# Five stage beginnings of a three-block network, worked row tile by row tile

## What is computed

```python
def rmsnorm_2(x, g):
    xf = x.astype(jnp.float32)
    y = xf * lax.rsqrt(jnp.mean(xf * xf, axis=-1, keepdims=True) + EPS)
    return (y * g.astype(jnp.float32)).astype(x.dtype)

def half_ffn(h, shift, scale, gate, g_pre, g_post, w13, w2):
    u = modulate_2(rmsnorm_2(h, g_pre), shift, scale)
    return h + 0.5 * gate * rmsnorm_2(swiglu(u, w13, w2), g_post)
```

## Time and profile before

| | us |
|---|---|
| median of 3 runs | 2326.73 |
| lowest and highest | 2322.61, 2327.68 |
| the profiled execution's own time | 2324.72 |
| its span, first to last instruction | 2323.3 |
| PE, DVE, ACT, POOL busy | 1982.9, 1008.2, 735.3, 42.6 |

### The profile page before, as it was taken

How to read it: one execution, slowest core, us unless ns; L and a number is a source line. 1 busy time by engine, 2 the same in 40 slices (tenths; PEclk the granted TensorE clock), 3 DMA queues, 4 the chain that set the end, 5 groups by cost and what they waited for, 6 DMA issues and landing times.

```text
span 2323.3 us, 28401 instructions
## 1 busy us (share of the span) xinstructions
PE 1982.9 (85%) x11830; PEld 1311.9 (56%) x11830; DVE 1008.2 (43%) x1713; ACT 735.3 (32%) x1196; POOL 42.6 (2%) x47
## 2 busy tenths in 40 slices
PE   6999777777877887777788799989999899999997
PEld 3556413332332433342444288868999788785786
DVE  3544222221221221222533367666664667653386
ACT  4333211111110111112111144454654554543365
POOL 0000000000000000000000000000000000000010
PEclk8998898989999999888799999999999999999999
DMA  9977999999999999999999955435345555250430
GB/s 399 419 310 264 405 392 410 417 413 414 413 414 414 416 413 412 416 411 408 410 410 409 405 188 192 168 102 170 112 143 175 165 178 185 95 203 19 145 118 19
DMA packets 210432, 672.03 MB, mean 289 GB/s; under 512 B 11504, under 2 KB 134512, under 8 KB 152192
## 3 DMA queue, kind: packets, MB, share of 16 engines
q1 hardware_dynamic: 210304, 670.21, 74.7%
HBM read 669.12 MB, written 1.05 MB: 288 GB/s over the span
## 4 chain that ended last, share of the span: by engine, by line
PE 50%; DMA 34%; DVE 11%; ACT 4%; issue 2%; SPq 0%; POOL 0%; DVEq 0%; ACTq 0%
DMA ring<-in_w 24%; PE pb L231 7%; PE pb L239 7%; PE pb L232 7%; PE pb L233 7%; DMA ring<-in_w_a 6%; PE pb L240 4%; DMA ring<-in_w_in 3%; DVE WB L333 3%; PE pb L1844 3%; PE pb L774 2%; PE pb L1869 2%; ACT WB L327 1%; DMA ring<-in_w_mod 1%; PE pb L3149 1%
## 5 line engine op out<-in xcount | busy, mean ns | idle before, releaser
L333 DVE TENSOR_TENSOR WB<-ring,WB 128x1024 fp32r<-128x1024 f32 (+3 forms) x370 | 426.1, 1193 | 465.4 <-ACT WB L327 465.1
L327 ACT ACTIVATE WB<-ring 128x1024 fp32r<-128x1024 f32 (+3 forms) x370 | 361.6, 1026 | 800.0 <-DMA ring<-in_w_a 463.3
L1844 PE MATMUL pb<-ring,big 128*32 128x512 f32 x2048 | 300.3, 679 | 147.1 <-DMA ring<-in_w 131.5
L231 PE MATMUL pb<-HHL,WB 128*128 128x256 f32 (+1 forms) x976 | 292.8, 300 | 11.8 <-DVE WB L333 4.3
L232 PE MATMUL pb<-HHL,WB 128*128 128x256 f32 (+1 forms) x976 | 284.2, 291 | 0.0
L233 PE MATMUL pb<-HHL,WB 128*128 128x256 f32 (+1 forms) x976 | 283.8, 291 | 0.0
L239 PE MATMUL pb<-HHL,WB 128*128 128x512 f32 x704 | 253.5, 404 | 1.7 <-DVE tmpT L643 1.4
L1844 PEld LDWEIGHTS pb<-ring,big 128*32 128x32 f32 x2048 | 46.8, 114 | 364.0 <-DMA ring<-in_w 275.3
L231 PEld LDWEIGHTS pb<-HHL,WB 128*128 128x128 f32 x976 | 195.1, 200 | 35.9 <-issue 20.6
L1869 PE MATMUL pb<-ring,big 128*32 128x512 f32 x1024 | 163.6, 649 | 49.5 <-DMA ring<-in_w 41.7
L240 PE MATMUL pb<-HHL,WB 128*128 128x256 f32 x704 | 198.9, 283 | 0.0
(11 more groups left out here) (467 smaller groups left out, 2268.2 us busy)
## 6 DMA issues: line engine op xcount, KB each, us to landing
ring<-in_w SPq DMA_DIRECT2D x384, 1024.0 KB, 16.5
ring<-in_w_a SPq DMA_DIRECT2D x66, 1024.0 KB, 13.3
ring<-in_w_in SPq DMA_DIRECT2D x38, 1024.0 KB, 10.0
ring<-in_w_ada SPq DMA_DIRECT2D x36, 1024.0 KB, 9.5
ring<-in_w_b SPq DMA_DIRECT2D x33, 1024.0 KB, 5.0
ring<-in_w_mod SPq DMA_DIRECT2D x24, 1024.0 KB, 11.6
ring<-in_w_out SPq DMA_DIRECT2D x8, 1024.0 KB, 5.2
ring<-in_b_w_in SPq DMA_DIRECT2D x8, 1024.0 KB, 6.3
```

The lines of the kernel that those rows point to most:

```text
L231: pe.matmul(o, l[0], r[0], start=start, stop=False)
L327: act.activation(WB[:, c % 2, 0, x:y], flat[:, x:y], ACT.Copy).then_inc(*A(("high", c, z)))
L333: dve.tensor_tensor(WB[:, c % 2, 1, x:y], flat[:, x:y], WB[:, c % 2, 0, x:y].bitcast(F32), ALU.subtract).then_inc(*V(("low", c, z), *([("f ...
L1844: e = pe.matmul(PB[half][32 * j:32 * j + 32, :], xeT[:, kk, 32 * x:32 * x + 32], s[:, 512 * j:512 * j + 512], start=kk == 0, stop=kk == 7)
```

## The change

At the five places the work is reordered by row tile. Tile 0's sum of squares is made by ACT and DVE in halves, then its norm, its 8 transposes, and eight gain-and-shift operations of 128 tokens each, all on DVE (L656 or L658 of the changed kernel). The high and low parts are made for four blocks at once (512 columns), low parts half by DVE and half by POOL (`low2`, L664). Tile 1 follows. PE multiplies tile 0 with the first chunk while tile 1's norm goes on, then tile 0 with the second chunk (in mx: tile 0 with both chunks first), then tile 1 with both. So the instructions on the first two chunks of fa and fb, on the first of mx and on the first two of b3 move half of the tokens each, and there are twice as many. The low part of the second chunk of each stage is made by POOL (`pool_split_half`, L338) and no longer by DVE. At three of the places the end of the stage before is woven in (`act_cross`, `dve_cross`). The first norm of the final output is also made tile by tile; it keeps its instructions otherwise.

```diff
-    def both_columns(pe, bank, hi, lo, kk):
-        pe.matmul(bank[:, :].rearrange("p (z t) -> p z t", z=2), hi, HHL[:, :, kk, 0:256], start=kk == 0, stop=False)
-        return pe.matmul(bank[:, 0:256], lo, HH[:, kk, 0:256], start=False, stop=kk == 7)
+    def both_columns(pe, bank, hi, lo, kk, x=0, n=256):
+        pe.matmul(bank[:, :].rearrange("p (z t) -> p z t", z=2)[:, :, x:x + n], hi, HHL[:, :, kk, x:x + n], start=kk == 0, stop=False)
+        return pe.matmul(bank[:, x:x + n], lo, HH[:, kk, x:x + n], start=False, stop=kk == 7)
...
+    SECOND = (s_ffa + 1, s_mix + 1, s_ffb + 1, s_3 + 1, s_3 + 13)
+
+    def act_split_half(act, c, z):
+        if z == 0:
+            act.wait_ge(*landed(("s", c)))
+            if c >= 2:
+                act.wait_ge(*at("used", c - 2))
+        x, y = halves_at(CH[c][1])[z]
+        act.activation(WB[:, c % 2, 0, x:y], slot(("s", c))[:, x:y], ACT.Copy).then_inc(*A(("high", c, z)))
...
+    def pool_split_half(pool, c, z):
+        x, y = halves_at(CH[c][1])[z]
+        pool.wait_ge(*at("high", c, z))
+        pool.tensor_tensor(WB[:, c % 2, 1, x:y], slot(("s", c))[:, x:y], WB[:, c % 2, 0, x:y].bitcast(F32), ALU.subtract).then_inc(
+            *G(("low", c, z), *([("free", ("s", c))] if z else [])))
...
+    def turn_bank(name, i, g):
+        return PB[(4, 5, 2, 3)[2 * i + g] if name == "mx" else 4 + 2 * i + g]
+
+    def pe_turn2(pe, name, xn, i):
+        for kk in range(8):
+            if kk % 4 == 0:
+                pe.wait_ge(*at("xn", name, i, kk // 4))
+            c = 128 * (kk % 4)
+            e = pe.transpose(turn_bank(name, i, kk // 4)[:, c:c + 128], xn(i)[:, kk * 128:kk * 128 + 128], ident)
+            if kk % 4 == 3:
+                e.then_inc(*P(("turn", name, i, kk // 4)))
...
+    def dve_turned2(dve, name, i, a, s, c0=0):
+        for kk in range(8):
+            g = kk // 4
+            if kk % 4 == 0:
+                dve.wait_ge(*at("turn", name, i, g))
+                if i:
+                    dve.wait_ge(*at("XT", name, 0, g))
+            src = turn_bank(name, i, g)[:, 128 * (kk % 4):128 * (kk % 4) + 128]
...
+                dve.tensor_scalar(quarter(g)[:, kk % 4, :], src, a(kk), s(kk), ALU.mult, ALU.add).then_inc(*V(("turned", name, i, kk)))
+        low2(dve, V, name, i, 0, c0)
...
+    def low2(e, done, name, i, g, c0=0):
+        x = slice(4 * g, 4 * g + 4), slice(c0 + 128 * i, c0 + 128 * i + 128)
+        e.wait_ge(*at("highT", name, i, g))
+        e.tensor_tensor(HL[:, x[0], x[1]], quarter(g), HH[:, x[0], x[1]].bitcast(F32), ALU.subtract).then_inc(*done(("XT", name, i, g)))
+
+    def pool_turn2(pool, name, c1, c0=0):
+        for i in range(2):
+            pool_split_half(pool, c1, i)
+            low2(pool, G, name, i, 1, c0)
...
+        squares(0, 1)
+        squares(0, 0)
+        root(0)
+        act_squares2(act, name, 0, xn(0)[:, 0:512], [("added", post, 0, 0)])
+        squares(1, 1)
+        act_root2(act, name, 0)
+        act_scale2(act, name, xn, 0)
+        act_split_half(act, c1, 0)
+        squares(1, 0)
+        root(1)
+        act_turned2(act, name, 0, c0)
+        act_squares2(act, name, 1, xn(1)[:, 0:512], [("added", post, 1, 0)])
+        act_split_half(act, c1, 1)
+        act_root2(act, name, 1)
+        act_scale2(act, name, xn, 1)
+        act_turned2(act, name, 1, c0)
+
...
+        add(0)
+        dve_squares2(dve, name, 0, xn(0)[:, 512:1024])
         product(1, 0)
+        dve_scale2(dve, name, xn, 0)
         product(1, 1)
-        add(0, 1)
-        dve_rstd(dve, (name, 1), st[:, 1:2])
-        dve.wait_ge(*last("v"))
-        add(1, 0)
-        add(1, 1)
+        dve_turned2(dve, name, 0, a, s, c0)
...
+        gain(0)
+        dve_squares2(dve, "fa", 0, xn(0)[:, 512:1024])
+        gain(1)
+        dve_scale2(dve, "fa", xn, 0)
+        dve_squares2(dve, "fa", 1, xn(1)[:, 512:1024])
+        dve_turned2(dve, "fa", 0, *fa.regions[0][2:])
+        dve_scale2(dve, "fa", xn, 1)
+        dve_turned2(dve, "fa", 1, *fa.regions[0][2:])
...
+                if q == 0 and kk % 4 == 0:
+                    pe.wait_ge(*at("XT", name, i, kk // 4))
+                for f in range(2):
+                    e = both_columns(pe, PB[2 * q + f], h[:, kk, 128 * f:128 * f + 128], l[:, kk, 128 * f:128 * f + 128], kk, 128 * i, 128)
+                    if i and kk == 7:
+                        e.then_inc(*P(("ffn", name, 0, q, f), *([("used", c)] if f else [])))
+
+        pe_turn2(pe, name, F.xn, 0)
+        first(0, 0)
+        pe_turn2(pe, name, F.xn, 1)
+        first(0, 1)
+        first(1, 0)
...
+        pe_turn2(pe, "mx", lambda i: xn_m[:, i, :], 0)
+        first(0)
+        first_rows(0)
+        pe_turn2(pe, "mx", lambda i: xn_m[:, i, :], 1)
+        first(1)
+        first_rows(1)
...
+        pe_turn2(pe, "a3", xn3, 0)
+        pe.wait_ge(*at("XT", "a3", "meta"))
+        first(0, TL[0:3:2])
+        pe_turn2(pe, "a3", xn3, 1)
+        first(1, TL[0:3:2])
+        first(0, TL[1:2])
+        first(1, TL[1:2])
+        first(2, TL[2::-1])
+        first(3, TL[2::-1])
...
+                    e = mm3(pe, PB[2 * q + f][:, c0:c1], (hi[:, kk, 128 * f:128 * f + 128], lo[:, kk, 128 * f:128 * f + 128]),
+                            XT(kk, c0, c1 - c0), kk == 0, kk == 7)
+                    if kk == 7 and c0:
+                        e.then_inc(*P(("u_in", q, f), *([("used", c)] if f else [])))
...
+        pe_turn2(pe, "b3", xn3, 0)
+        pe.wait_ge(*at("XT", "b3", "meta"))
+        first_columns(0, 0, 144)
+        pe_turn2(pe, "b3", xn3, 1)
+        first_columns(1, 0, 144)
+        first_columns(0, 144, 272)
+        first_columns(1, 144, 272)
+        for p in range(2, 4):
```

More of the change, by code:

```diff
@@ L598, in act_roots2, with act_squares2 @@
+    def act_squares2(act, name, i, junk, waits, s0=16):
+        s = st[:, s0 + i:s0 + i + 1]
+        for w in waits:
             act.wait_ge(*at(*w))
         act.wait_ge(*last("a"))
-        act.activation(junk[0], X[:, 0, :], ACT.Square, scale=1.0 / 32, accum_out=s[0]).then_inc(*A())
-        act_root(act, ("norm", name, 0), s[0])
-        for w in x_from(1, 0):
-            act.wait_ge(*at(*w))
+        act.activation(junk, X[:, i, 0:512], ACT.Square, scale=1.0 / 32, accum_out=s).then_inc(*A())
@@ new lines, in act_scale2, with act_turned2, high @@
+    def act_scale2(act, name, xn, i):
+        act.wait_ge(*at("rstd", ("norm", name, i)))
+        act.activation(xn(i)[:, 512:1024], X[:, i, 512:1024], ACT.Copy, scale=st[:, 16 + i:17 + i]).then_inc(*A(("xn", name, i, 1)))
+    def act_turned2(act, name, i, c0=0):
+        def high(g):
+            c = c0 + 128 * i
+            act.activation(HH[:, 4 * g:4 * g + 4, c:c + 128], quarter(g), ACT.Copy).then_inc(*A(("highT", name, i, g)))
+        for g in range(2):
+            act.wait_ge(*at("turned", name, i, 4 * g + 3))
+            high(g)
@@ new lines, in pool_turn2, with act_cross, squares, root @@
+    def pool_turn2(pool, name, c1, c0=0):
+        for i in range(2):
+            pool_split_half(pool, c1, i)
+            low2(pool, G, name, i, 1, c0)
+    def act_cross(act, post, banks, name, xn, c1, c0=0):
+        def squares(i, j):
+            if j:
+                act.wait_ge(*at("rows", post, i))
+            else:
+                act.wait_ge(*at("product", post, i, 0))
+            act.wait_ge(*last("a"))
+            act.activation(mraw[:, :], PB[banks[2 * i + j]][:, :], ACT.Square, scale=1.0 / 32,
+                           accum_out=st[:, 8 + 2 * i + j:9 + 2 * i + j]).then_inc(*A(("post", post, i, j)))
+        def root(i):
+            act.wait_ge(*at("eps", post, i))
+            act.wait_ge(*last("a"))
+            act.activation(st[:, i:i + 1], st[:, 8 + 2 * i:9 + 2 * i], ACT.Sqrt, bias=st[:, 9 + 2 * i:10 + 2 * i]).then_inc(*A(("root", (post, i))))
+        act_ready(act)
+        squares(0, 1)
[14 more added lines that the diff above has]
+        act_turned2(act, name, 1, c0)
@@ L696, in product, with add @@
             dve.tensor_tensor(tmp[2 * i + j], PB[banks[2 * i + j]][:, :], row[:, 512 * j:512 * j + 512], ALU.mult).then_inc(
-                *V(("product", name, i, j), *(ends if i and j else [])))
-        def add(i, j):
-            x = X[:, i, 512 * j:512 * j + 512]
-            dve.scalar_tensor_tensor(x, tmp[2 * i + j], st[:, i:i + 1], x, ALU.mult, ALU.add).then_inc(*V(("added", name, i, j)))
+                *V(("product", post, i, j), *(ends if i and j else [])))
+        def add(i):
+            dve_rstd(dve, (post, i), st[:, i:i + 1])
+            dve.wait_ge(*last("v"))
+            for j in range(2):
+                x = X[:, i, 512 * j:512 * j + 512]
+                dve.scalar_tensor_tensor(x, tmp[2 * i + j], st[:, i:i + 1], x, ALU.mult, ALU.add).then_inc(*V(("added", post, i, j)))
@@ L2058, in dve_experts, with gain @@
                 dve_scaled(dve, "ctx", TLC, xn_c)
-        for i in range(2):
-            add(15, i)
-        dve_squares2(dve, "xf", big[:, 5120:5632], 24)
-        for i in range(2):
```

(15 more changed lines are left out.)

311 lines of the change are left out of this document (136 added, 175 removed).

## The result

The changed kernel takes 2369.56 us, the median of 5 runs (2367.71 to 2373.88), against 2326.73 for the kernel before: a ratio of 1.0197, with a 95% interval of 1.0183 to 1.0210. That is 42.8 us slower. The forecast was slower by 25, with a range that ends at 2362. The sign held, and so did the price of a narrow matmul; the waits and the clock of two of the five beginnings did not.

The account below looks back on a forecast made before the run. PE was taken as the bound once a stage has begun. Terms of +5.4 (fa), +4.1 (mx), +3.9 (fb), -0.8 (a3) and +12.6 (b3) sum to 25.2 us, giving a forecast of 2351 us, range 2338 to 2362.

Parts of the forecast that it names:

- The sign: Whole kernel: the change makes it slower, chance 0.95.
- the price of a narrow matmul: PE, first two chunks: a narrow matmul costs about 0.115 us, as much as one of 256 columns.
- a3's term: Beginning of a3: the earlier start slightly outweighs PE's wait for tile 1, -0.8 us, between -1.6 and +0.1.
- The bound: All stages: once a stage has begun PE sets its pace, so time lost at a beginning goes through to the end.
- Rival 4: Behind the beginnings PE does not set the pace, so b3's 12.6 us would be swallowed by DVE's work: 2338, chance 0.02.
- Rival 1: Narrow matmuls cost their columns: 2331 to 2336, or about 2340 at 81 ns each; chance 0.10 with the 81 ns.
- rival 2: Not slower: matmul price below about 0.07 us, tile 1's chain unblocked, clock up at first product: -2 us, 2323, chance 0.05.
- POOL blocks DVE: At the beginnings POOL's new splitting holds up DVE: tile 1 scaled at 17.2 instead of 14.1, worth 2 us in the sum.
- operand at 10.1: Beginning of mx: tile 0's first operand is ready 10.1 us after the closing norm's first product, as in fb.
- rival 3: At the beginnings the clock stays or falls low, 3 to 5 us more half clock each: 2357 to 2363, chance 0.13.
- some 16 of 48 narrow products at 0.213, 32 at 0.115: Beginning of b3: tile 0's products run partly at half clock, until 16.6 us; b3's whole term was +12.6 us.

Follow-up runs that it names:

- e8: The kernel before, with identity transposes filling PE ahead of the real ones at the five beginnings (40 each, 12 in b3): 2322.51 us, ratio 0.9992.
- e1: The changed kernel with the beginning of b3 alone as before the change: 2353.52 us, ratio 1.0116.
- e9: The changed kernel with identity transposes on PE in b3, 8 ahead of tile 0's real transposes and 33 behind them: 2361.13 us, ratio 1.0155.
- e6: The changed kernel with 24 identity transposes on PE in b3, between tile 0's transposes and its first product: 2369.01 us, ratio 1.0188.

## Why the forecast was wrong, and where it was right

The landmarks of all profiled executions, in us, each the mean of the executions counted; the new order is that of the changed kernel without further edits in that stage, and those as before include e8 with its filling:

| part | as before (executions) | new order (executions) | difference | forecast |
|---|---|---|---|---|
| fa's start to mx | 198.4 (3) | 204.1 (11) | +5.7 | +5.4 |
| mx's beginning | 23.4 (6) | 38.3 (5) | +14.9 | +4.1 |
| behind it, to fb | 270.5 (6) | 272.8 (8) | +2.3 | 0 |
| fb's start to a3 | 199.0 (4) | 203.7 (10) | +4.7 | +3.9 |
| a3's start to b3 | 186.8 (2) | 186.8 (12) | 0.0 | -0.8 |
| b3's beginning | 22.1 (6) | 37.5 (5) | +15.4 | +12.6 |

Some rows scatter: fa's part from 197.5 to 200.2 and from 203.4 to 205.4, mx's new beginning from 37.0 to 40.3, a3's part from 183.8 to 188.9 in the new order. So a3's term of 0.8 us can't be told from none, and that the sum of 43.0 meets the 42.8 of the medians so closely is in part chance.

The forecast of 25.2 lacks 10.8 in mx, 2.8 in b3, 2.3 behind mx, and 1.9 in the rest. Told by cause, and worked out below for the one profiled execution, it lacks a wait of ACT in mx (5.9 us) and half clock beyond what it had reckoned with: 1.3 and 3.2 us in mx, 3.2 in b3.

- **The bound held.** What PE ends later at a beginning goes through to the end: putting b3 and mx back as they were gives 16 and 12 us in the medians, for 15.4 and 14.9 in the stages. And from the end of b3's beginning to the last instruction all 14 executions take 90.1 to 91.1 us, whatever b3 took. Rival 4 is out.
- **The price of a narrow matmul held.** Forecast 0.115, and 0.23 a pair. In b3, 16 intervals of 128 columns take 2277.54 - 2275.75 = 1.79 us (the two rows above), 0.112 each, and the pairs of fa and fb lie 0.23 apart. The Trainium skill (TensorE: Matmul & The Clock Gate, section Back-to-back issue gap) has about 81 ns; the measurement decides against it here, for products with float32 operands and a new stationary block each. Rival 1 is out with it, and so is rival 2.
- **fa and fb** came within 0.8 us of their terms. PE's last pairs stand at 31.4 in fa (1366.02 - 1334.66; forecast 31.6) and 29.05 in fb (29.2).
- **POOL blocks DVE**, as forecast: DVE's scaling of half a row (L645) takes 2.12 us in fb and 2.11 in mx beside POOL's L338, and 0.49 in mx once L338 stands elsewhere. The Trainium skill's rule (SBUF — State Buffer, section Who interferes with whom) is that a DVE instruction in a two-port mode and a GpSimd instruction exclude each other for a whole instruction, whichever came first; the times agree (L338 ends at 1867.00, L645 at 1867.29), but no row names the mode. It cost less than the 2 us it was given: PE, with its narrow products, was late for tile 1 anyway (for its scaled row PE waits 0.46 us in fb, and in fa, mx and b3 not at all).
- **mx is the step that failed,** in two terms. The first is "operand at 10.1", taken over from fb's chain; it came at 16.0, so 5.9 us. The reason was in the list of edits and was not priced: the split that was moved ahead on ACT's queue waits for a landing, and in mx that chunk is issued only when the closing norm's last product has freed its slot. In the kernel before the same transfer was issued 4.1 us into the stage and split behind everything:

```profile
1532.96 1.48 SPq L224 DMA_DIRECT2D ring<-in_w_in  x3
...
1544.21 3.89 ACT L327 ACTIVATE WB<-ring 128x1024 fp32r<-128x1024 f32 x4
```

The new order on DVE also puts that last product, and so the issue, 2.4 us later (6.5 us into the stage). That alone is not it: ACT is at the split at 6.1, and a transfer issued at 4.1 that takes 5.3 us would still have kept it for some 3 us, an estimate from these rows. In fa, fb, a3 and b3 the chunk had landed.

- **The second term of mx is the clock.** The forecast had tile 0's products in 7.7 us (10.1 to 17.8) and tile 1's in 5.6 (until 27.5). Tile 0's took 9.05, because the clock came back 7.4 us behind the first product and not 4.6, and tile 1's 8.8, because it fell a second time: 1.3 and 3.2 us more. With the 5.9 that is the 10.4 by which this execution's 37.9 exceeds 27.5. The wait for tile 1 between them came as forecast (2.99 us for about 3), and it is the one that rival 3 named. The length of the second low stretch is also what makes the new beginning of mx scatter: tile 1's products take 7.3 us in e1, where it takes 37.0, and 10.1 in e9, where it takes 40.3.
- **b3 was mis-sized:** "some 16 of 48 narrow products at 0.213, 32 at 0.115". All 48 ran at half clock, 0.213 apart, and the transposes behind them too: 32 x 0.1 = 3.2 us more. That and mx's second term are rival 3's mechanism, at two of the five places; rival 3 had 0.13. The measured time lies above its upper end of 2363 by about the wait on ACT, which it did not have.
- **Left open:** the 2.3 us behind mx. The time from there to fb's start takes few values (269.1, 270.7, 272.3, 273.7 to 273.8); six of the eight executions with a new mx are at the highest, but one at the lowest. Nor is it shown why the clock fell at 2251.9 in e6 with PE busy; only that in e9, with both gaps ahead filled, it did not.

No kernel here beats the one before; a3's part alone equals it.
